# Modulation bundles moved between the stages of a two-block transformer kernel, and the values moved to the end of an attention step

## The chip, the cores and the metric

The kernel runs on one core of one Trainium2 chip. The metric is the device time of one execution in microseconds (us). Its parts are TensorE (PE in the profile, with PEld for its weight loads), VectorE (DVE), ScalarE (ACT), GpSimd (POOL) and SyncE (SP). SP issues the loads of the weights, POOL those of the modulation. All work is in fp32; most products are made of high and low parts of both operands, three products for one.

## What is computed

One sequence of 256 positions with 1024 features goes through two blocks.

```python
# block 1
h = rmsnorm(x, ln1)
qkv_a, z_a, b_a, a_a, q_b, k_b, v_b = split(h @ w_in)
y_a = gated_deltanet(qkv_a, z_a, b_a, a_a, ...)      # 4 heads of 128, chunks of 64, a triangular solve in each
y_b = dilated_attention(q_b, k_b, v_b)               # 8 heads of 64
x = x + concat([y_a, y_b]) @ w_out
h = rmsnorm(x, ln2)
x = x + (silu(causal_dwconv(h @ w_gate)) * (h @ w_up)) @ w_down      # 1024 -> 2816 -> 1024
x = rmsnorm(x, ln_f)
# block 2, layers i = 0 and 1
mod = silu(c) @ ada_w[i] + ada_b[i]                  # c [1, 1024], ada_w[i] [1024, 6144]
sh1, sc1, g1, sh2, sc2, g2 = split(mod, 6)
h = rms_norm(x, norm_mix_g[i]) * (1.0 + sc1) + sh1
y = diff_attention(h, ...) if i == 0 else chunked_attention(h, ...)   # 8 heads with 2 maps; 16 heads
x = x + g1 * y
h = rms_norm(x, norm_ffn_g[i]) * (1.0 + sc2) + sh2
x = x + g2 * grouped_moe(h, ...)                     # 16 experts of 512, 2 of them for each position
```

## The kernel before

**Units.** Every dense weight of block 1 and of the attentions goes through TensorE in units of 512 KB (128x1024 fp32). SP loads them six ahead: unit c waits until the low part of unit c-6 is made. ScalarE makes the high part (`whi`, L545), DVE the low part (`wlo`, L551), TensorE the products (L561). The units of `w_in` are those of Q and K (0 to 7), V, the gates G, and Z; `w_used` counts the units that TensorE is done with, and `U_V`, `U_FFN` and `U_WO` are the numbers at which the units of V, of the FFN and of the attention's output begin. The experts' weights of the MoE go through a ring of their own, without units.

**Bundles.** The product silu(c) @ ada_w of both layers doesn't depend on x. It is cut into 48 bundles, six groups of eight (8 chunks of the 1024 inputs). A bundle is 1 MB: `load_ada` issues two loads of 512 KB each on POOL's queue (L494). `ada_bundle` uses it in four matmuls of 128x512 whose output has 32 rows (eight records with the two passes of fp32, L506), summed in the bank `ADA_BANK[group]`. TensorE uses the bundles strictly in the order of their numbers, and `ada(to)` in its program means: all up to `to` now. Groups 0, 3 (g1 and g2 of a layer) end in `grow_add`, the others in `acol_copy`, a copy by ScalarE that frees the bank.

A bundle has a place, by the table of `ADA_PLACE`. Bundles 0 to 11 share two places in `ering`; the others up to `ADA_BLOCK` share three, the third of which is `a_raw`, laid over the tiles in which block 1's input of `w_out` is split (`a_hi`, `a_lo`). `load_ada` waits for `ada_used`, that is until the bundle that had the place before is used. Bundles from `ADA_BLOCK` on (`ADA_TAIL`) lie in places of the work buffer, which are free from the end of the delta rule on; places 13 and 14 are `a_raw` again.

```python
ADA_BLOCK = 24
ADA_TAIL = [0, 1, 2, 0, 1, 2, 0, 1, 2, 10, 11, 12, 0, 1, 2, 10, 12, 13, 14, 12, 13, 14, 12, 13]
ADA_PLACE = [n % (2 if n < ADA_LATE else 3) for n in range(ADA_BLOCK)] + ADA_TAIL
ADA_NORM, ADA_STEP, ADA_LASTS, ADA_FFN = 27, 30, 32, 40
```

**TensorE's order.** It is written out by hand, and so is that of the other engines; they meet at semaphores. Each engine runs its own list strictly in order. TensorE's, with times of the profile: the units of Q, K and V (10 to 60 us); the dilated attention (phase 0) with the units of G and bundles 0 to 5 beside it (to 121); Z with bundles 6 and 7 (to 141); the delta rule, whose triangular solve is a chain of small products, each waiting for DVE or ScalarE (144 to 199): bundles 8 to 13 stand ahead of its loop over the levels n = 1 to 5, 14 to 23 in it, two in each level; then the finale of the delta rule (L1819, L1825 and the groups of four `heads`, L1831; to 213) with no bundles; the turn of y (L718) and the eight units of `w_out` (L561, from 215.9); bundles 24 to 26 (`ADA_NORM`); the FFN's 22 steps (248 to 447), with bundles 27, 28, 29 behind steps 0, 1, 2, and 30 and 31 (`ADA_LASTS`) ahead of the last `down_pe`; bundles 32 to 39 (`ADA_FFN`) behind it; the last norm of block 1 and the turn 3 of its result; QKV of layer 0 (465 to 535); its attention, phase 1, one head in each of eleven overlapped steps (536 to 580), with bundles 40 to 47 one in a step; `w_o` (588 to 607), MoE (628 to 855); then layer 1 in the same way (856 to 1236). `busy(bank, 11)` (L1088) is eleven products of constants that only keep TensorE working; it stands ahead of turn 6, in layer 1 alone.

**POOL's order.** It issues bundles 0 and 1 once unit 3 has landed (`raw_in[3]`), then eight small loads of the bias rows (`grow`, L1592), then bundles 2 to 23, each at its wait. From the finale on: 24 to 29, `mod_spread(0)` (`mrow`, L1602), 30 to 35, the relative position tables (`t_rows`, `rel_rows`), 36 to 40, a mask (L1631), and when `w_o`'s units begin to be used up, 41 to 44; 45 to 47 stand between its partial sums of squares (L1642 to L1646) in the attention's last steps.

**DVE in phase 1.** A step of `attention_dve` has `largest(i)` (bias and maximum of both maps' scores, L933 to L938), `sums(i - 1)` (L958 to L964) and `values(i - 3)`: the division of the value product, which TensorE makes in L873, with its copy into `hn` (L980). `values` waits for that product (`pv_ps`). In phases 0 and 1 it stands at the head of the step, in phase 2 at its end.

## Time and profile before

| | |
|---|---|
| Median of the runs | 1237.31 us (1234.36, 1237.31, 1240.54) |
| Profiled execution, its own time | 1238.61 us |
| Span of the profiled execution | 1236.8 us, mean granted clock 0.978 |
| PE busy | 1111.0 us (90%) |
| PEld busy | 744.5 us (60%) |
| DVE busy | 593.5 us (48%) |
| ACT busy | 433.3 us (35%) |
| POOL busy | 94.7 us (8%) |
| Chain that ended last | PE 68%, DMA 16%, DVE 10%, ACT 4%, issue 2% |
| Bytes moved | 356.14 MB, mean 288 GB/s |

The profile is one execution. The busy time of an engine is an average over stages with different limits, so the chain that ended last, followed back from the last instruction, tells which work set the time in each stretch. In a row of a timeline the bracket is the idle time of the engine ahead of the instruction and what ended it. The records of one line that follow each other are drawn together (x8); when they overlap, the time is from the first start to the last end. PEclk is the granted clock of TensorE as a share of the full one.

### The profile page before, as it was taken

How to read it: one execution, taken by the hardware profiler on the slowest of the kernel's cores; microseconds unless marked ns; L12 is line 12 of the kernel's file. 1: busy time of each engine (PE TensorE's matmuls, PEld its weight loads, DVE VectorE, ACT ScalarE, POOL GpSimd, SP SyncE). 2: the span in 40 equal slices, each digit the busy share in tenths (PEclk: the TensorE clock that was granted, in tenths of full speed). 3: DMA queues.
4: the chain of work that ended last, by engine and by line, in shares of the span. 5: the costliest groups of instructions: out<-in, count | busy, mean ns of one | idle time of the engine just before them, and what ended most of it. 6: DMA issues, size and time to landing. Idle time of an engine off the chain costs nothing.

```text
span 1236.8 us, 17354 instructions
## 1 busy us (share of the span) xinstructions
PE 1111.0 (90%) x6770; PEld 744.5 (60%) x6770; DVE 593.5 (48%) x1175; ACT 433.3 (35%) x738; POOL 94.7 (8%) x189
## 2 busy tenths in 40 slices
PE   6899786999999989976999999987999999999986
PEld 6787455789999947844754343424887754343422
DVE  3378464566666647736532322225765532232223
ACT  5444522454455446435331120103545441020100
POOL 2010130232000010022000000001000000000000
PEclk9999999989999999988999999999999999999998
DMA  9855693799777774683579999997675479999995
GB/s 292 241 162 198 230 324 143 254 320 339 225 228 223 230 254 137 232 335 131 201 297 409 409 409 409 409 409 283 216 273 207 138 284 410 409 409 409 409 409 217
DMA packets 163983, 356.14 MB, mean 288 GB/s; under 512 B 10425, under 2 KB 79289, under 8 KB 163777
## 3 DMA queue, kind: packets, MB, share of 16 engines
q1 hardware_dynamic: 146864, 295.81, 65.9%
q0 software_dynamic: 17024, 59.26, 13.7%
q8 instruction: 51, 0.84, 0.3%
q14 instruction: 28, 0.22, 0.0%
q10 hardware_dynamic: 16, 0.02, 0.0%
HBM read 351.89 MB, written 7.36 MB: 290 GB/s over the span
## 4 chain that ended last, share of the span: by engine, by line
PE 68%; DMA 16%; DVE 10%; ACT 4%; issue 2%; POOL 0%; SPq 0%; DVEq 0%; ACTq 0%
PE bank L561 35%; PE bank L1112 12%; DMA ering<-in_moe_w_up 9%; PE bank L1123 8%; DMA a_raw<-in_ada_w 3%; PE bank L1080 3%; DVE wlo L551 2%; PE bank L506 2%; DMA wraw<-in_w_in 1%; DMA ering<-in_ada_w 1%; ACT whi L545 1%; PE bank L718 1%; PE bank L858 1%; PE bank L1184 1%; DVE work L2267 1%
## 5 line engine op out<-in xcount | busy, mean ns | idle before, releaser
L551 DVE TENSOR_TENSOR wlo<-wraw,whi 128x1024 fp32r<-128x1024 f32 x150 | 179.4, 1222 | 65.3 <-ACT whi L545 62.9
L545 ACT ACTIVATE whi<-wraw 128x1024 fp32r<-128x1024 f32 x150 | 153.9, 1054 | 60.9 <-PE bank L561 49.6
L561 PE MATMUL bank<-a_hi,whi 128*128 128x256 f32 x512 | 149.2, 291 | 5.8 <-DVE wlo L551 4.7
L561 PE MATMUL bank<-a_lo,whi 128*128 128x256 f32 x512 | 147.4, 288 | 0.0
L561 PE MATMUL bank<-a_hi,wlo 128*128 128x256 f32 x512 | 147.2, 288 | 0.0
L1112 PE MATMUL bank<-ering,work 128*64 128x512 f32 x592 | 134.0, 595 | 12.2 <-DMA ering<-in_moe_w_up 11.0
L1313 DVE TENSOR_TENSOR work<-work,bank 128x512 f32<-128x512 f32 x16 | 11.0, 688 | 208.7 <-PE bank L1112 208.7
L561 PEld LDWEIGHTS bank<-a_hi,whi 128*128 128x128 f32 x512 | 101.1, 197 | 14.0 <-issue 6.9
L561 PE MATMUL bank<-whi,a_hi 128*128 128x512 f32 x256 | 102.1, 399 | 5.7 <-DVE a_lo L748 3.0
L1221 ACT ACTIVATE o_hi<-work 128x512 fp32r<-128x512 f32 x32 | 20.2, 632 | 236.8 <-DVE work L1281 236.4
L1112 PEld LDWEIGHTS bank<-ering,work 128*64 128x64 f32 x592 | 41.2, 137 | 102.7 <-issue 79.7
L561 PEld LDWEIGHTS bank<-a_lo,whi 128*128 128x128 f32 x512 | 100.9, 197 | 0.7
L561 PEld LDWEIGHTS bank<-a_hi,wlo 128*128 128x128 f32 x512 | 100.8, 197 | 0.0
L561 PE MATMUL bank<-wlo,a_hi 128*128 128x512 f32 x256 | 100.5, 392 | 0.0
L561 PE MATMUL bank<-whi,a_lo 128*128 128x512 f32 x256 | 100.3, 392 | 0.0
L1123 PE MATMUL bank<-ering,work 128*64 128x512 f32 x352 | 78.5, 596 | 1.1 <-DVE work L1316 1.1
L1281 DVE SCALAR_TENSOR_TENSOR work<-bank,sm,mrow 128x512 f32<-128x512 f32 x32 | 22.6, 747 | 91.7 <-PE bank L1123 91.7
L561 PEld LDWEIGHTS bank<-whi,a_hi 128*128 128x128 f32 x256 | 48.4, 189 | 17.9 <-issue 7.4
L1209 ACT ACTIVATE work<-bank,mcol 128x256 f32<-128x256 f32 x64 | 31.6, 561 | 70.0 <-PE bank L1080 70.0
L561 PEld LDWEIGHTS bank<-whi,a_lo 128*128 128x128 f32 x256 | 48.5, 189 | 10.3
L561 PEld LDWEIGHTS bank<-wlo,a_hi 128*128 128x128 f32 x256 | 48.5, 189 | 9.8 <-issue 0.2
L1123 PEld LDWEIGHTS bank<-ering,work 128*64 128x64 f32 x352 | 24.2, 137 | 46.7 <-issue 44.4
(313 smaller groups left out, 1823.8 us busy)
## 6 DMA issues: line engine op xcount, KB each, us to landing
ering<-in_moe_w_down SPq DMA_DIRECT2D x44, 1024.0 KB, 18.4
ering<-in_moe_w_up SPq DMA_DIRECT2D x42, 1024.0 KB, 18.5
ering<-in_moe_w_gate SPq DMA_DIRECT2D x32, 1024.0 KB, 18.2
ering<-in_ada_w POOLq DMA_DIRECT2D x40, 512.0 KB, 5.8
work<-in_ada_w POOLq DMA_DIRECT2D x38, 512.0 KB, 7.5
work<-in_moe_w_gate SPq DMA_DIRECT2D x16, 1024.0 KB, 16.7
wraw<-in_w_in SPq DMA_DIRECT2D x28, 512.0 KB, 5.8
wraw<-in_a_w_qkv SPq DMA_DIRECT2D x24, 512.0 KB, 4.6
```

The costliest lines, as they stand in the source:

```text
L506: mm = nc.tensor.matmul(psum[ADA_BANK[g]][32 * q:32 * q + 32, :], silc[:, k, :], ada_part(n, q // 2)[:, (q % 2) * HALF:(q % 2 + 1) * HALF] ...
L545: nc.scalar.activation(w_hi(c), wraw[:, c % RING, :], ACT.Copy).then_inc(w_hi_done, 1)
L551: nc.vector.tensor_tensor(w_lo(u[0]), wraw[:, u[0] % RING, :], w_hi(u[0]).bitcast(F32), ALU.subtract).then_inc(w_lo_done, 1)
L561: mm = nc.tensor.matmul(out_ap, l, r, start=first and n == 0, stop=last and n == len(terms) - 1)
L718: tr = nc.tensor.transpose(turn_bank(turn, b)[:, (2 * kk + t) * P:(2 * kk + t + 1) * P], src[:, t, cols(2 * b + kk)], ident)
L858: tr = nc.tensor.transpose(psum[4 + n % 2][:, b * P:(b + 1) * P], scr[:, slot, b * P:(b + 1) * P], ident)
L1080: mm = nc.tensor.matmul(bank[:, kk * S:kk * S + cols], part[:, t, pair_cols(2 * b + kk)], sel[:, t, 0:cols // PAIR_SLOTS, :], start=n == 1 ...
L1112: mm = nc.tensor.matmul(bank[rows, :], x_e[:, k, rows], w[:, e, kk * HALF:(kk + 1) * HALF], start=first and kk == 0, stop=last and kk == 1)
L1123: mm = nc.tensor.matmul(psum[4 + half][rows, :], hid_t[:, m % 4, rows], w[:, e, half * HALF:(half + 1) * HALF], start=first, stop=last)
L1209: ins = nc.scalar.activation(xe[:, :, k, :], gather_bank(g, b)[:, kk * S:(kk + 1) * S].rearrange("p (a c) -> p a c", a=2), ACT.Identity, b ...
L1221: nc.scalar.activation(o_hi[:, cols], o_f[:, cols], ACT.Copy).then_inc(e_o_hi, 1)
L1281: return nc.vector.scalar_tensor_tensor(out=o_f[:, cols], in0=psum[4 + half][:, :], scalar=sm[:, M_GS:M_GS + 1], in1=mrow[:, 1, cols], op0 ...
```

## The change

- **Bundles 24 to 31 in block 1.** `ADA_BLOCK` is 32: these eight go through the three places of the ring too. TensorE's bundles 12 and 13 now stand behind the kk products, 14 and 15 behind m1, two in each level of the loop, 26 and 27 behind the products L1819 and L1825 (L1823 and L1830 in the changed file), 28 to 31 between the groups of heads.
- **Those behind move up.** `ADA_NORM` is 35, `ADA_LASTS` 37, `ADA_FFN` 40: 32 to 34 ahead of the FFN's norm, none between the FFN's steps, 35 and 36 ahead of the last `down_pe`, 37 to 39 behind it. `busy(psum[4], 11)` then stands ahead of the turn in layer 0 too. The attention keeps 40 to 47, one in a step.
- **Places and loads.** Bundle 41 gets a new place 15, which is `hn`, and is loaded when turn 3 has read `hn`. POOL loads 32 to 34 ahead of `mod_spread(0)`, 35 to 40 right behind it, 41 at the mask, 42 to 45 where 41 to 44 were, 46 and 47 between its sums.
- **First loads.** Bundles 0 and 1 wait for the eighth unit's products (`w_used` at `U_V`) and no longer for the landing of unit 3.
- **Banks and copies.** Group 3 sums in bank 7, group 4 in bank 2. `acol_copy(0)` stands ahead of the loop over the levels, `acol_copy(1)` at n = 5. `grow_add(1)` moves on DVE from the norm behind the FFN to block 1's turn, and TensorE waits for it ahead of the last bank of `w_out`'s first unit.
- **Values last.** In phase 1 `values(i - 3)` stands at the end of the step, as in phase 2.

```diff
@@ -122,14 +122,14 @@
 ADA_N = 8 * len(ADA_GROUPS)
-ADA_BANK = [7, 7, 7, 2, 3, 7]
+ADA_BANK = [7, 7, 7, 7, 2, 7]
 ADA_LATE = 12
-ADA_BLOCK = 24
-ADA_TAIL = [0, 1, 2, 0, 1, 2, 0, 1, 2, 10, 11, 12, 0, 1, 2, 10, 12, 13, 14, 12, 13, 14, 12, 13]
+ADA_BLOCK = 32
+ADA_TAIL = [0, 1, 2, 0, 1, 2, 10, 11, 12, 15, 13, 14, 12, 13, 14, 12]
 ADA_PLACE = [n % (2 if n < ADA_LATE else 3) for n in range(ADA_BLOCK)] + ADA_TAIL
-ADA_NORM, ADA_STEP, ADA_LASTS, ADA_FFN = 27, 30, 32, 40
+ADA_NORM, ADA_LASTS, ADA_FFN = 35, 37, 40
@@ -470,7 +470,7 @@
-            return {10: 3, 11: 4, 12: 5, 13: 3, 14: 4}.get(ADA_PLACE[n], ADA_PLACE[n])
+            return {10: 3, 11: 4, 12: 5, 13: 3, 14: 4, 15: 0}.get(ADA_PLACE[n], ADA_PLACE[n])
@@ -479,6 +479,8 @@
             place = ADA_PLACE[n]
+            if place == 15:
+                return hn[:, h, :]
             if place >= 3:
@@ -499,8 +501,8 @@
                 pe.wait_ge(grow_done, 1)
-            elif n == 16:
-                pe.wait_ge(acol_done, 1)
+            elif n in (16, 24):
+                pe.wait_ge(acol_done, n // 8 - 1)
             pe.wait_ge(ada_in[ada_ring(n)], 32 * ada_turn(n))
@@ -576,7 +578,7 @@
-        def unit_rows(pe, u, lhs_hi, lhs_lo, banks, first, last):
+        def unit_rows(pe, u, lhs_hi, lhs_lo, banks, first, last, last_bank=None):
@@ -584,6 +586,8 @@
                     h, l = w_hi(u[0])[:, cols], w_lo(u[0])[:, cols]
+                    if last_bank is not None and t + half == 2:
+                        last_bank()
                     mm = products(banks[t * 2 + half][:, :], [(lh, h), (lh, l), (ll, h)], first, last)
@@ -982,7 +986,7 @@
             for i in range(units + 3):
-                if ph < 2 and i >= 3:
+                if ph == 0 and i >= 3:
                     values(i - 3)
@@ -990,7 +994,7 @@
                     between(i)
-                if ph == 2 and i >= 3:
+                if ph != 0 and i >= 3:
                     values(i - 3)
@@ -1583,7 +1587,7 @@
-            pool.wait_ge(raw_in[3], 16)
+            pool.wait_ge(w_used, U_V)
             load_ada(pool, 0)
@@ -1605,11 +1609,11 @@
             nc.gpsimd.memset(fg[:, :, 0:2], 0.0).then_inc(pads_zero, 1)
-            for n in range(ADA_BLOCK, ADA_STEP):
+            for n in range(ADA_BLOCK, ADA_NORM):
                 load_ada(pool, n)
...
             mod_spread(0)
-            for n in range(ADA_STEP, ADA_STEP + 6):
+            for n in range(ADA_NORM, ADA_FFN + 1):
                 if ADA_PLACE[n] == 10:
@@ -1630,11 +1634,11 @@
-            for n in range(ADA_STEP + 6, ADA_FFN + 1):
-                load_ada(pool, n)
+            pool.wait_ge(tr_done, 4 * 4)
+            load_ada(pool, ADA_FFN + 1)
             toe_mask(0)
             pool.wait_ge(w_used, U_WO[0])
-            for n in range(ADA_FFN + 1, ADA_FFN + 5):
+            for n in range(ADA_FFN + 2, ADA_FFN + 6):
                 load_ada(pool, n)
@@ -1645,8 +1649,8 @@
                                         ).then_inc(sub_done, 1)
-                if ADA_FFN + 5 + n < ADA_N:
-                    load_ada(pool, ADA_FFN + 5 + n)
+                if ADA_FFN + 6 + n < ADA_N:
+                    load_ada(pool, ADA_FFN + 6 + n)
@@ -1772,7 +1776,7 @@
                 mm.then_inc(kk_ps, 1)
-            ada(13)
+            ada(14)
@@ -1780,7 +1784,7 @@
                 tr.then_inc(m1_ps, 1)
-            ada(14)
+            ada(16)
@@ -1805,12 +1809,12 @@
                     blocks(psum[3 * c], mb[c], ym[c]).then_inc(n_ps, 1)
-                ada(13 + 2 * n)
+                ada(15 + 2 * n)
                 for c in range(2):
...
                     blocks(psum[3 * c + 2], nm[c], xm[c]).then_inc(xyn_ps, 1)
-                ada(14 + 2 * n)
+                ada(16 + 2 * n)
@@ -1819,12 +1823,14 @@
                 mm.then_inc(n_ps, 1)
+            ada(27)
             for c in range(2):
...
                 mm.then_inc(xyn_ps, 1)
+            ada(28)
@@ -1834,14 +1840,18 @@
             heads(psum[6], lambda h: y_all[0][:, h, :], lambda h: bv[0][:, h, :], fin_ps)
+            ada(29)
             pe.wait_ge(fin_copied, 1)
...
             heads(psum[0], lambda h: aqk[0][:, h, :], lambda h: v0[:, h, :], fin_ps)
+            ada(30)
             pe.wait_ge(fin_copied, 2)
...
             heads(psum[2], lambda h: qkv_t[:, h, P:S], lambda h: s1[:, h, :], fin_ps)
+            ada(31)
             pe.wait_ge(fin_r, 1)
             heads(psum[3], lambda h: y_all[1][:, h, :], lambda h: r1[:, h, :], fin_ps)
+            ada(32)
             pe.wait_ge(fin_copied, 3)
@@ -1861,18 +1871,16 @@
                 chunk_ready(pe, 1, k)
-                unit_rows(pe, (U_WOUT + n, None, 0), a_hi[:, k, :], a_lo[:, k, :], psum[4:8], n == 0, n == KC - 1)
+                unit_rows(pe, (U_WOUT + n, None, 0), a_hi[:, k, :], a_lo[:, k, :], psum[4:8], n == 0, n == KC - 1,
+                          (lambda: pe.wait_ge(grow_done, 2)) if n == 0 else None)
             mod_columns(psum[3])
...
             step_pe(pe, 0, None, 0, turn=2)
-            ada(ADA_NORM + 1)
             step_pe(pe, 1, None, 0, first=True)
-            ada(ADA_NORM + 2)
             step_pe(pe, 2, None, 0)
-            ada(ADA_STEP)
@@ -1895,8 +1903,7 @@
                 pe.wait_ge(x_done, X_AT["ffn"] if l == 0 else X_AT["moe", 0])
-                if l == 1:
-                    busy(psum[4], BUSY_MOD)
+                busy(psum[4], BUSY_MOD)
                 turn = 3 + 3 * l
@@ -1919,7 +1926,6 @@
-                        pe.wait_ge(grow_done, 2)
                         pe.wait_ge(acol_done, 3)
@@ -2091,12 +2097,12 @@
                 nc.scalar.activation(dec[c], dec[c], ACT.Exp, scale=-1.0).then_inc(dec_exp, 1)
+            acol_copy(0)
             for n in range(1, len(LEVELS)):
-                if n in (2, LAST):
-                    acol_copy(0 if n == 2 else 1)
                 if n in (3, 4):
...
                 if n == 5:
+                    acol_copy(1)
                     for t in range(T):
@@ -2460,6 +2466,7 @@
             turn_lo(dve, 1, vec[:, V_Y1:V_Y1 + 8], EARLY)
+            grow_add(1)
             for c in range(2):
@@ -2538,8 +2545,6 @@
                     nc.vector.memset(v_one[:, :, :, 64:65], 1.0)
-                else:
-                    grow_add(1)
...
```

**TensorE, end of the delta rule.** L1800 is the last level's products; `ering` and `a_raw` are a bundle's places; L1819 and L1825 close the levels, L1831 is the finale, L718 the turn ahead of `w_out`. Before:

```order
L506 MATMUL bank<-ering,silc 32x512 x4
L1800 MATMUL bank<-work 64x64 x32
L506 MATMUL bank<-a_raw_55,silc 32x512 x2
L506 MATMUL bank<-a_raw_56,silc 32x512 x2
L1819 MATMUL bank<-work 64x64 x8
L1825 MATMUL bank<-work 64x64 x8
L1831 MATMUL bank<-work 128x128 x4
L1831 MATMUL bank<-work,mrow 128x128 x4
L1831 MATMUL bank<-work 128x128 x20
L718 MATMUL bank<-con,hn 128x128 x8
```

After (all lines are some lower in the file; L508 is the bundle):

```order
L1823 MATMUL bank<-work 64x64 x8
L508 MATMUL bank<-a_raw_55,silc 32x512 x2
L508 MATMUL bank<-a_raw_56,silc 32x512 x2
L1830 MATMUL bank<-work 64x64 x8
L508 MATMUL bank<-ering,silc 32x512 x4
L1837 MATMUL bank<-work 128x128 x4
L508 MATMUL bank<-ering,silc 32x512 x4
L1837 MATMUL bank<-work,mrow 128x128 x4
L1837 MATMUL bank<-work 128x128 x4
L508 MATMUL bank<-a_raw_55,silc 32x512 x2
L508 MATMUL bank<-a_raw_56,silc 32x512 x2
L1837 MATMUL bank<-work 128x128 x8
```

Where the finale had no bundle, six stand in or just ahead of it now (26 to 31; the last two follow below the rows).

**POOL, from the finale on.** `work`, `a_raw` and `hn` are the bundles' places, `mrow` the spread rows. Before:

```order
L1607 MEMSET work 128x2x2
L494 DMA work<-in_ada_w 128x1024 x12
L1602 DMA mrow<-grow_74 32x512 x16
L494 DMA work<-in_ada_w 128x1024 x12
L1620 DMA t_rows<-t_by_distance 128x512 x8
L1624 DMA rel_rows<-in_b_rel_bias 128x513 x16
L494 DMA work<-in_ada_w 128x1024 x10
L1631 MEMSET work 64x8x64
L494 DMA a_raw_55<-in_ada_w 128x1024 x2
L494 DMA a_raw_56<-in_ada_w 128x1024 x2
L494 DMA work<-in_ada_w 128x1024 x2
L494 DMA a_raw_55<-in_ada_w 128x1024 x2
```

After:

```order
L1611 MEMSET work 128x2x2
L496 DMA work<-in_ada_w 128x1024 x6
L1606 DMA mrow<-grow_74 32x512 x16
L496 DMA work<-in_ada_w 128x1024 x12
L1624 DMA t_rows<-t_by_distance 128x512 x8
L1628 DMA rel_rows<-in_b_rel_bias 128x513 x16
L496 DMA hn<-in_ada_w 128x1024 x2
L1635 MEMSET work 64x8x64
L496 DMA a_raw_55<-in_ada_w 128x1024 x2
L496 DMA a_raw_56<-in_ada_w 128x1024 x2
L496 DMA work<-in_ada_w 128x1024 x2
L496 DMA a_raw_55<-in_ada_w 128x1024 x2
```

Six loads (three bundles) stand ahead of the spread where twelve stood, twelve behind it, and the ten behind the tables are gone but for the two into `hn`.

**DVE, phase 1, end of its step 2 and start of its step 3.** L960 and L964 end the sums of a head, L980 is its values, L933 and L935 read the next scores. Before:

```order
L960 SCALAR_TENSOR_TENSOR sm_76<-sm_76 128x2
L964 SCALAR_TENSOR_TENSOR work_77<-work_77,sm_76 128x128
L964 SCALAR_TENSOR_TENSOR work_77<-work_77,sm_76 128x256
L980 TENSOR_TENSOR hn_67<-bank6,sm_76 128x2x128
L933 ISA work_77,sm_76<-bank2,work_77 128x128
L933 ISA sm_76 128x1
L935 ISA work_77,sm_76<-bank2,work_77 128x256
L935 ISA sm_76 128x1
```

After:

```order
L964 SCALAR_TENSOR_TENSOR sm_76<-sm_76 128x2
L968 SCALAR_TENSOR_TENSOR work_77<-work_77,sm_76 128x128
L968 SCALAR_TENSOR_TENSOR work_77<-work_77,sm_76 128x256
L937 ISA work_77,sm_76<-bank2,work_77 128x128
L937 ISA sm_76 128x1
L939 ISA work_77,sm_76<-bank2,work_77 128x256
L939 ISA sm_76 128x1
L942 TENSOR_SCALAR sm_76<-sm_76 128x2
```

The first values stood ahead of the scores of step 3; they now stand behind its sums. So at each border of steps DVE now does the values of the head before the one it did there.

## Rows read from the trace of the kernel before

**Rows 1.** The chain of waits, 169 to 200 us. Columns: start us, us, what.

```profile
169.52 6.43 DMA a_raw<-in_ada_w
...
177.91 9.70 DMA a_raw<-in_ada_w
...
189.57 8.80 DMA a_raw<-in_ada_w
198.41 1.07 PE bank L506 x8
```

**Rows 2.** Windows: stretch, length, busy PE, PEld, DVE, ACT, POOL, PEclk, DMA share, GB/s.

```profile
40.00:45.00 5.00, 5.00 (x34) 5.00 (x34) 2.81 (x3) 0.85 (x2) 0.00 (x0) 0.74 0.98 260
155.00:165.00 10.00, 8.99 (x88) 6.36 (x80) 6.92 (x15) 0.00 (x0) 3.82 (x8) 0.83 0.85 291
165.00:177.00 12.00, 10.24 (x226) 6.58 (x226) 6.71 (x18) 4.02 (x7) 3.53 (x7) 1.00 0.97 330
...
198.00:216.00 18.00, 11.63 (x105) 9.77 (x106) 9.27 (x19) 6.57 (x13) 0.00 (x0) 1.00 0.00 1
...
535.00:560.00 25.00, 15.72 (x110) 8.58 (x110) 12.60 (x68) 12.06 (x46) 9.16 (x18) 0.86 0.96 379
```

**Rows 3.** Timeline of TensorE: start, us, line, operation, tiles, xcount [idle before <-releaser].

```profile
39.56 0.55 PE L561 MATMUL bank<-a_hi,whi 128*128 128x256 f32 x1 [4.67 <-DVE wlo L551]
...
210.82 1.13 PE L1831 MATMUL bank<-work 128*128 128x128 f32 x8 [1.10 <-DVE sm L2451]
...
215.86 0.47 PE L561 MATMUL bank<-whi,a_hi 128*128 128x512 f32 x1 [3.04 <-DVE a_lo L748]
...
556.85 1.07 PE L506 MATMUL bank<-work,silc 128*32 128x512 f32 x8 [1.07 <-DMA work<-in_ada_w]
...
573.89 1.06 PE L506 MATMUL bank<-a_raw,silc 128*32 128x512 f32 x8
...
856.50 2.72 PE L1088 MATMUL bank<-con 128*128 128x128 f32 x22 [1.20 <-DVE x_res L1304]
```

**Rows 4.** The chain of waits over the whole run, columns as in Rows 1.

```profile
18.29 17.85 DMA wraw<-in_w_in
...
258.71 0.99 PE bank L506 x8
...
450.30 9.06 DMA work<-in_ada_w
...
465.06 22.01 PE bank L561 x96
...
859.39 1.16 ACT hn L660
...
863.93 22.01 PE bank L561 x96
```

**Rows 5.** DMA queue (packets, MB, share), 0 to 65 us; an issue, 66 to 68.

```profile
q0 software_dynamic: 832, 2.62, 12.4%
...
ering<-in_ada_w POOLq DMA_DIRECT2D x2, 512.0 KB, 4.3
```

**Rows 6.** Timeline of POOL, columns as in Rows 3.

```profile
14.51 2.26 POOL L494 DMA_DIRECT2D ering<-in_ada_w  x4 [12.67 <-DMA wraw<-in_w_in]
...
183.62 1.05 POOL L494 DMA_DIRECT2D ering<-in_ada_w  x2 [2.70 <-PE bank L506]
```

**Rows 7.** Timeline of DVE, columns as in Rows 3.

```profile
182.27 2.35 DVE L551 TENSOR_TENSOR wlo<-wraw,whi 128x1024 fp32r<-128x1024 f32 x2
...
212.06 0.69 DVE L2459 TENSOR_TENSOR work<-work,bank 128x512 f32<-128x512 f32 x1 [0.78 <-PE bank L1831]
...
555.81 0.42 DVE L980 TENSOR_TENSOR hn<-bank,sm 128x256 f32<-128x256 f32 x1 [1.31 <-PE bank L873]
...
560.32 0.42 DVE L980 TENSOR_TENSOR hn<-bank,sm 128x256 f32<-128x256 f32 x1 [1.31 <-PE bank L873]
```

**Rows 8.** Timeline of ScalarE, columns as in Rows 3.

```profile
454.52 1.15 ACT L660 ACTIVATE hn<-x_res,sm 128x1024 f32<-128x1024 f32 x1 [0.23 <-DVE sm L683]
```

## The prediction

> **What bounds the kernel now.** I read the chain of waits first, whole and then by stretch. It is TensorE's own work for 68% of the span and transfers for 16%, so I looked for the places in which the modulation bundles stand on it, since these are what the change moves. There are five. (1) In the delta rule's chain (166 to 199 us) one place of the bundle ring, `a_raw`, is all that counts: load, use, next load, three times over [rows 1]. In its first part TensorE is busy 10.24 of 12 us, the DMA share is 0.97 [rows 2]. Then comes the finale, in which no byte moves (198 to 216 us: 1 GB/s) [rows 2], and the first `w_out` unit at 215.86 [rows 3]. (2) At the start TensorE stands still for 4.67 us before unit 6 [rows 3], and the chain shows a transfer of 17.85 us that ends last [rows 4]. (3) In the FFN the chain is TensorE's work without a gap, so each bundle between the steps costs its own length, 0.99 us [rows 4]. (4) Behind the FFN eight bundles are done, and their transfers stand on the chain with 9.06 us [rows 4]. (5) In the first attention of block 2 bundle 43 is waited for 1.07 us [rows 3], and in each step of 4.51 us DVE waits 1.31 for TensorE's value products before it takes the next scores [rows 7].
>
> **Start: bundles 0 and 1 and the bias rows wait for unit 7.** POOL issues them from 14.5 us on [rows 6], among the first units of `w_in`. They are 2.62 MB and hold all 16 engines for 12.4% of 65 us, 8.06 us [rows 5]. Unit 7 lands at 36.14 (18.29 + 17.85) [rows 4]; behind it in ScalarE's and DVE's order stand the small split and unit 6's low part. With 8.06 us less ahead it lands at about 28. TensorE comes to unit 6 by its own work at 34.9 (39.56 - 4.67) [rows 3], so the whole stall goes, and the slow stretch behind it with it: the granted clock is 0.74 from 40 to 45 us [rows 2], 5 x 0.26 = 1.3. Sum -6.0. What is next: the same bytes come at about 41 us, beside units loaded six units ahead, and bundle 0 is used at 65. Ends -6.5 and -3.
>
> **Chain: bundles 24 to 31 in it.** TensorE's 1.07 us for each [rows 1] lies in the waits; what counts is the transfer. Bundles share three places, each loaded when the bundle three before is used. The hops of `a_raw` are 8.39 (169.52 to 177.91), 11.66 (to 189.57) and 10.71 us (to 198.41 + 1.07 + 0.8 for the next issue) [rows 1]. Three bundles pass in a hop: 2.80, 3.89, 3.57 us for one. In the second and the third a megabyte of weight units goes along, in the first none, and the late ones have none either (1 GB/s in 198 to 216) [rows 2]: I take 2.80, 22.4 for eight. By the rate of 165 to 177 us, 330 GB/s [rows 2], it would be 3.17 and 25.4. The earlier bundles are asked for sooner (two ahead of the level loop, where one stood), and from 155 to 165 us the share is 0.85 [rows 2], which is 1.5 us of room: with a little behind it 2 us. So the last one lands at 198.4 + 22.4 - 2 = 218.8. Behind it stand its own 1.07, one group of heads, the turn, `a_hi` and `a_lo`, 215.86 - 210.82 = 5.04 [rows 3]: `w_out` begins at 224.9, **+9.0**. At x us for a bundle the term is 8x - 13.4: +12.0 at 3.17, +17.8 at 3.89; below, 379 GB/s (535 to 560 us) [rows 2] is 2.77, and with 3 us of room +7.8. Queued behind each late bundle on TensorE are the heads, behind those ScalarE's copies and DVE's norm; all of the finale but its end is covered. `grow_add(1)` is one DVE operation like that of 0.69 us [rows 7] behind `a_lo`; TensorE asks for it only at the unit's fourth bank, after nine products: nothing.
>
> The row of 379 GB/s over 25 us [rows 2] can be set against a rule. The Trainium skill (page DMA: Bandwidth & Descriptors, section Where 436 GB/s comes from) says that a core's HBM side binds at about 358 GB/s. By that rule a bundle would be 2.93 us and the term +10.1; the row is above the page's figure, so the row stands.
>
> **FFN steps.** Three bundles between steps 0, 1 and 2 go, 0.99 us each [rows 4]: -3.0. TensorE remains the bound. Six bundles' loads now go out in one burst at about 243 to 250 us, 6.3 MB, 17 us at 370 GB/s, beside the FFN's first units. These are loaded six units ahead; I take no stall, and up to +3.
>
> **Behind the FFN.** After the last step's products three bundles are left, loaded long before, then eleven filler products (22 records, 2.72 us in the other layer) [rows 3], then the norm is next in line: ScalarE's half of `hn` ends at 454.52 + 1.15 = 455.67 [rows 8]. In the other layer, where only the norm stands ahead, the first unit begins 863.93 - 860.55 = 3.4 us behind it [rows 4]: here 459.06, against 465.06 [rows 4]. **-6.0**, ends -6.5 and -5.
>
> **First attention of block 2.** Bundle 41 lies in `hn` long before, so the transfers from 535 us on serve bundles 42 and later, each used one step later; they still come at the pace of the bytes, with a share of 0.96 [rows 2]. Bundle 44 comes when 43 came, 556.85 [rows 3], in step 4 and not in step 3. With the values last DVE doesn't wait 1.31 us in each step [rows 7]; 4.51 - 1.31 = 3.2, I take 3.3 for the handovers. Bundle 47 ends at 556.85 + 1.07 + 3 x 3.3 = 567.8, before at 573.89 + 1.06 = 574.95 [rows 3]: **-7.1**. The tail, in which POOL's partial sums now stand ahead of the last values, I leave as long as before, to 1 us. Ends -9 and -4. The MoE stages behind are paced by transfers that begin when `w_o` is done, so they move along.
>
> **Sum**, against the profiled execution (1238.61, span 1236.8): -6.0 + 9.0 - 3.0 - 6.0 - 7.1 = -13.1, 1225.5. The median of the runs, 1237.31, is 1.3 below it; the difference from that gives 1224.2, **1224**.
>
> **The rivals.** *A, dear bundles:* each costs 3.89 us as in the second hop, +17.8, the total is -4.3, **1233**. For it: two hops of three were of that size. Against it: the short one is the only one without other traffic. *B, gains taken back:* the moved loads stall the weight units at 41 and at 250 us, and the attention stays at the pace of its transfers past step 4: -2 + 9 + 0 - 6 - 4 = -3, **1234**. *C, slower, at the end of the delta rule:* the ring doesn't keep three loads in flight, because POOL's queue is held at the wait for the oldest place. A load alone lands in 4.3 us [rows 5]; with its second issue, the use and the handover 6.4 us if quite serial, +37.8 for the term and +15.7 in all, **1253**. It is slower from 4.4 us a bundle on, by over 0.5% from 5.2. Against it: three were in flight in every hop shown. *D, POOL is held by DVE:* if each of the 16 late issues waited for one DVE operation of 0.69 us [rows 7], 11 us come on top, **1235**. Against it: POOL's pair at 183.62 took 1.05 us [rows 6] while DVE ran two operations of 2.35 us with two inputs from the same memory [rows 7]. The Trainium skill (page SBUF — State Buffer, section SBUF: two separate sides) states such a lock: DVE's hold on the shared ports keeps POOL from writing descriptors. By that rule D would be the likely case; the pair's row doesn't show it. *E, every term at its good end:* -6.5 + 7.8 - 3 - 6.5 - 9 = -17.2, **1220**.
>
> **How the numbers follow.** Forecast 0.60, A 0.12, B 0.10, C 0.05, D 0.05, E 0.08. 0.5% is 6.2 us, about what a measurement of this kernel can tell from no change: faster ends at 1231.1, slower begins at 1243.5. Faster: forecast, E and a quarter of A and B, 0.73; slower: C and a little of B, 0.06; the rest, 0.21, is the same. The range holds forecast, E, A, B and D: **1217 to 1235**.
>
> **What the profile of the changed kernel would show.** Start: no idle time at unit 6. Chain: past bundle 23 hops of 8 to 9 us, with bytes where there were none, and `w_out` at about 219 (224.9 less the start's 6). FFN: no gap. Behind it: filler, and no transfer between FFN and turn. Attention: no idle time of DVE before the values, steps of 3.3 us. I am wrong if the late hops are over 10 us, if weight units stall at 41 or 250 us, or if the steps stay at 4.5.

## The result

The changed kernel takes 1223.34 us (median of 4 runs, 1221.25 to 1225.48) against 1238.92 us of the kernel before, measured beside it: a ratio of 0.9880, 95% interval 0.9846 to 0.9914, or 11 to 19 us less. By the half per cent that the prediction sets as its border this is faster. The forecast was 1224 us in a range of 1217 to 1235, and 13.1 us less. A second set of the changed kernel (`after_again`, 6 runs, median 1224.35) gave 0.9897 (0.987 to 0.9925); one execution of the kernel before in that set, of 3847.78 us, is left out of the ratio as a slow one.

The profiled execution took 1223.52 us, its span is 1221.7. On the page, the kind of chain hardly changed:

```profile
span 1221.7 us, 17399 instructions
...
PE 68%; DMA 15%; DVE 10%; ACT 4%; issue 2%; POOL 0%; SPq 0%; ACTq 0%; DVEq 0%; POOLq 0%
```

**By stage.** A stage ends where TensorE begins the next one (rows of its timeline and of the chain). Times are us. Both kernels were profiled twice; the second profiles are of `before_again` and `after_again` (below).

| Stage | before | before, second | after | after, second | forecast |
|---|---|---|---|---|---|
| to the first product of the gates | 141.15 | 142.68 | 134.89 | 134.36 | -6.0 |
| to the loop over the levels | 25.38 | 25.63 | 28.68 | 28.55 | |
| the loop | 32.88 | 33.91 | 33.70 | 35.62 | |
| finale and turn, to `w_out` | 16.45 | 16.46 | 21.35 | 21.13 | +9.0 (these three) |
| to the FFN's loop | 65.11 | 63.81 | 61.96 | 60.59 | -3.0 |
| the loop of the FFN | 161.59 | 161.59 | 161.59 | 161.60 | 0 |
| to QKV of layer 0 | 22.50 | 22.38 | 16.95 | 16.94 | -6.0 |
| QKV | 71.25 | 71.26 | 71.24 | 72.24 | 0 |
| attention, to its turn | 48.52 | 47.56 | 40.72 | 40.66 | -7.1 |
| from there to the MoE of layer 1 | 422.8 | 423.9 | 422.9 | 422.3 | 0 |
| the last MoE and the output | 229.18 | 229.04 | 227.73 | 226.63 | 0 |

**The chain of the changed kernel** (start us, us, what), against [rows 4]:

```profile
34.74 10.55 PE bank L563 x76
...
198.19 6.28 DMA ering<-in_ada_w
204.51 1.06 PE bank L508 x8
205.58 1.98 PE bank L1837 x16
207.56 0.99 PE bank L508 x8
208.56 1.98 PE bank L1837 x16
...
231.46 12.29 DMA wraw<-in_w_up
...
255.16 23.73 PE bank L563 x168
...
454.12 1.16 ACT hn L664
...
459.12 22.02 PE bank L563 x96
...
850.27 22.05 PE bank L563 x96
```

The transfer of 17.85 us at the start is gone; unit 6 starts at 34.74 with no idle time (the forecast said 34.9 for TensorE's own pace). Ahead of the FFN's norm a transfer of `w_up` now ends last, at 243.75; from the first unit of `w_out` to the FFN's first product it is 36.5 us instead of 36.0. The FFN's first steps are one piece, without bundles. QKV begins at 459.12, where the forecast had 459.06 with nothing moved ahead of the FFN's end; that end did move by only 0.4 us, since start, chain and FFN steps nearly cancel.

**Windows** (stretch, length, busy PE, PEld, DVE, ACT, POOL, PEclk, DMA share, GB/s), against [rows 2]: the slow stretch behind the start, the ring's stretch, and its end.

```profile
35.00:40.00 5.00, 5.00 (x44) 5.00 (x43) 1.67 (x2) 1.61 (x4) 0.00 (x0) 1.00 1.06 292
156.00:208.00 52.00, 41.96 (x704) 24.96 (x696) 21.18 (x46) 12.96 (x23) 17.38 (x34) 0.93 1.01 370
208.00:219.00 11.00, 7.96 (x66) 5.32 (x59) 8.17 (x14) 4.04 (x8) 0.00 (x0) 1.00 0.31 114
```

**TensorE's timeline at the end of the delta rule**, against [rows 3]. The idle time is in brackets, with what ended it.

```profile
194.26 2.08 PE L1804 MATMUL bank<-work 64*64 64x64 f32 x64 [1.37 <-ACT work L2114]
...
199.13 1.07 PE L508 MATMUL bank<-a_raw,silc 128*32 128x512 f32 x8 [0.43 <-DMA a_raw<-in_ada_w]
...
201.99 1.07 PE L508 MATMUL bank<-ering,silc 128*32 128x512 f32 x8 [0.72 <-DMA ering<-in_ada_w]
...
204.51 1.06 PE L508 MATMUL bank<-ering,silc 128*32 128x512 f32 x8 [0.36 <-DMA ering<-in_ada_w]
...
207.49 1.07 PE L508 MATMUL bank<-a_raw,silc 128*32 128x512 f32 x8
...
210.47 1.07 PE L508 MATMUL bank<-ering,silc 128*32 128x512 f32 x8
...
212.55 1.06 PE L508 MATMUL bank<-ering,silc 128*32 128x512 f32 x8
...
218.62 0.47 PE L563 MATMUL bank<-whi,a_hi 128*128 128x512 f32 x1 [3.04 <-DVE a_lo L752]
```

The rows from 199.13 on, but the last, are bundles 26 to 31. The last one that waits for its transfer is 28, at 204.51, and for 0.36 us. Bundles 29 to 31 lie ready. So in this profile, and in the second of the changed kernel, the ring sets the time up to about 205, and from there on it is TensorE's own order. In other profiles of the same delta rule bundles 30 and 31 are waited for too (a table below). The wait for ScalarE at 194.26 is new.

Ahead of the loop over the levels, the loop's first products in the kernel before, then bundle 15 and the same products in the changed kernel:

```profile
166.53 1.15 PE L1800 MATMUL bank<-work 64*64 64x64 f32 x32 [2.54 <-DVE work L2400]
```

```profile
161.71 1.93 PE L508 MATMUL bank<-ering,silc 128*32 128x512 f32 x8 [2.29 <-DMA ering<-in_ada_w]
163.57 1.83 PE L1804 MATMUL bank<-work 64*64 64x64 f32 x32
```

TensorE waited there for DVE; it now waits for bundle 15, and then bundle and products take 1.93 and 1.83 us instead of the 1.06 and 1.15 of other rows: the granted clock is 0.53 from 161.7 to 165.3 us. In the loop it is 0.63 from 185.2 to 189.8, behind a wait of 2.69 us for bundle 22.

### The profile page after: what moved, and what is told of

It is laid out like the page before. It is cut to its first block, busy times and chain, and to the rows that moved or that the text cites. A ratio compares the mean times of both kernels' runs of the same rounds, so it can differ in the third digit from the quotient of the medians.

```text
span 1221.7 us, 17399 instructions
## 1 busy us (share of the span) xinstructions
PE 1115.8 (91%) x6792; PEld 748.3 (61%) x6792; DVE 593.3 (49%) x1175; ACT 432.2 (35%) x738; POOL 94.5 (8%) x189
## 4 chain that ended last, share of the span: by engine, by line
PE 68%; DMA 15%; DVE 10%; ACT 4%; issue 2%; POOL 0%; SPq 0%; ACTq 0%; DVEq 0%; POOLq 0%
PE bank L563 35%; PE bank L1116 12%; DMA ering<-in_moe_w_up 9%; PE bank L1127 8%; DMA ering<-in_ada_w 3%; PE bank L1084 3%; PE bank L508 2%; DVE wlo L553 2%; DMA work<-in_ada_w 1%; ACT whi L547 1%; DMA wraw<-in_w_up 1%; PE bank L722 1%; PE bank L835 1%; PE bank L1188 1%; DVE work L2273 1%
## 5 line engine op out<-in xcount | busy, mean ns | idle before, releaser
L1116 PE MATMUL bank<-ering,work 128*64 128x512 f32 x592 | 134.0, 596 | 11.7 <-DMA ering<-in_moe_w_up 11.0
L563 PEld LDWEIGHTS bank<-whi,a_hi 128*128 128x128 f32 x256 | 48.5, 190 | 16.8 <-issue 6.4
L1213 ACT ACTIVATE work<-bank,mcol 128x256 f32<-128x256 f32 x64 | 31.6, 560 | 70.0 <-PE bank L1084 70.0
L563 PEld LDWEIGHTS bank<-wlo,a_hi 128*128 128x128 f32 x256 | 48.5, 190 | 9.8 <-issue 0.2
```

The costliest lines, as they stand in the source:

```text
L563: mm = nc.tensor.matmul(out_ap, l, r, start=first and n == 0, stop=last and n == len(terms) - 1)
L1116: mm = nc.tensor.matmul(bank[rows, :], x_e[:, k, rows], w[:, e, kk * HALF:(kk + 1) * HALF], start=first and kk == 0, stop=last and kk == 1)
L1213: ins = nc.scalar.activation(xe[:, :, k, :], gather_bank(g, b)[:, kk * S:(kk + 1) * S].rearrange("p (a c) -> p a c", a=2), ACT.Identity, b ...
```

## The experiments

Each is an edit of the changed kernel, unless its name says otherwise. Ratios are to the kernel before, measured beside the run.

**Is it the transfers? `few_bytes`**

```diff
+                cut = 8 if 24 <= n < 32 else D
-                nc.gpsimd.dma_start(ada_part(n, h), a["ada_w_2"][l][k * P:(k + 1) * P, j * D:(j + 1) * D]
+                nc.gpsimd.dma_start(ada_part(n, h)[:, 0:cut],
+                                    a["ada_w_2"][l][k * P:(k + 1) * P, j * D:j * D + cut]
```

> Bundles 24 to 31 load 8 of their 1024 columns (their sums are wrong by that), all else as in the changed kernel: the bytes of these eight are gone, TensorE's matmuls stay. Theory T (the transfers through the three places set the end of the delta rule): w_out begins 4 to 6 us earlier, at 213 to 215 instead of 218.6, and the last waits for bundles go; the rest of the 9.0 is TensorE's own time between the heads. Rival P (TensorE's own eight times 1.07 us set it, the transfers are hidden behind them): w_out begins within 1 us of 218.6.

Timeline of TensorE, the last two bundles and the first unit:

```profile
208.21 1.06 PE L510 MATMUL bank<-ering,silc 128*32 128x512 f32 x8
...
210.30 1.07 PE L510 MATMUL bank<-ering,silc 128*32 128x512 f32 x8
...
216.36 0.47 PE L565 MATMUL bank<-whi,a_hi 128*128 128x512 f32 x1 [3.04 <-DVE a_lo L754]
```

`w_out` begins at 216.36, 2.3 us before the changed kernel and 3.3 before its second profile; from the gates on it is 82.3 us against 83.7 and 85.3. The finale alone is 19.6 us instead of 21.3. Neither theory is right as it stood: by these profiles eight megabytes are worth 1.4 to 3 us, since TensorE's own order is close behind them. The part differs by as much from one profile of the changed kernel to the next, so only this is sure: they are not worth the 9.0. Median 1220.15, ratio 0.987 (0.9833 to 0.9908), which overlaps with the interval of `after_again` in the same set.

**And TensorE's part? `one_product`**

```diff
-            for q in range(4):
+            for q in ([3] if 24 <= n < 32 else range(4)):
```

> Bundles 24 to 31 keep all their bytes, but TensorE makes one of their four matmuls (three quarters of their sums are left out): 8 x 0.75 = 6 us less of TensorE. Theory T: the waits for the transfers take most of it, w_out begins 1 to 2 us earlier than 218.6. Rival P: 5 to 6 us earlier.

One of its bundles at the place of the one at 212.55:

```profile
213.27 1.04 PE L508 MATMUL bank<-ering,silc 128*32 128x512 f32 x2
```

The experiment didn't take away what it should. One matmul with an output of 32 rows lasts 1.04 us with its two passes; the four of a whole bundle last 1.06 us together. So they run side by side, each in another 32 rows of the output bank. 0.02 us of TensorE for each bundle was gone and not 0.75, `w_out` begins at 219.31, and the median is 1226.87 (0.9899). That agrees with what the Trainium skill (page TensorE: Matmul & The Clock Gate, section Part 3: Packing small matmuls — row/col tiling) says of matmuls whose outputs lie in different 32-row strips. The expectation had each of the four at a quarter of the bundle's time.

**What do the eight cost altogether? `neither`** has the edit of `few_bytes`, one matmul for each of these bundles, and 8 columns in it.

> Bundles 24 to 31 load 8 columns and TensorE makes one matmul of 8 columns for each instead of four of 512 (their sums are left out): what the eight cost in the chain altogether. Both theories: w_out begins 9.0 us earlier than in the changed kernel, at 209.6 (by the sum in the prediction). If it begins at 211 or later, part of the 9.0 was not the eight bundles, but the places and the moved copies.

`w_out` begins at 218.24, not at 209.6. Window of the finale, columns as above, and one of its groups of heads:

```profile
197.20:207.72 10.52, 9.58 (x58) 8.70 (x56) 1.28 (x4) 1.95 (x4) 3.88 (x8) 0.50 0.06 3
```

```profile
204.22 2.07 PE L1840 MATMUL bank<-work,mrow 128*128 128x128 f32 x8 [0.48 <-ACT work L2122]
```

With the bundles nearly gone the granted clock was 0.50 in this stretch, the lower of TensorE's two levels, and the same heads took 2.07 us that took 1.16 in the changed kernel, whose finale was granted 1.00. The finale was 21.8 us, and the gain was lost in it. Up to the finale nothing changed: 28.67 and 33.71 us in the two parts ahead of it, as in the changed kernel. So the 3.3 us ahead of the loop are no matter of bundles 24 to 31. Two more of the earlier ones stand ahead of it now, eight for six, and this is the likely reason, but no run takes them back alone. Median 1221.42, ratio 0.9878 (0.9843 to 0.9914). What the eight cost altogether this run can't say, since the clock took the gain.

**Is 16.45 us for the finale of before a chance? `before_again`** is the kernel before.

> The kernel before once more, for a second profile of its delta rule. Its finale took 16.45 us in the first profile, at a granted clock of 1.00. Theory C (that was a chance: without bundles in it the finale mostly runs at a lower clock, as in the other profiles without them): 19 us or more, clock 0.5 to 0.8. Theory T (it is 16.5 us as a rule, and the eight bundles made it 4.9 us longer): 16 to 17 us, clock 1.00.

Windows of the finale without bundles, in the kernel before, in its second profile, and in `before_values` (below), whose delta rule is the same:

```profile
199.40:215.90 16.50, 10.54 (x101) 9.51 (x97) 8.63 (x17) 6.57 (x13) 0.00 (x0) 1.00 0.00 0
```

```profile
202.20:218.70 16.50, 10.55 (x101) 9.50 (x97) 8.94 (x18) 6.56 (x13) 0.00 (x0) 0.99 0.00 0
```

```profile
200.30:219.60 19.30, 13.35 (x101) 12.20 (x97) 8.62 (x17) 6.56 (x13) 0.00 (x0) 0.82 0.00 0
```

Theory C falls: the finale is 16.5 us at the full clock in two of three. But the third had 0.82 and took 2.8 us more with the same instructions. The difference of 4.9 us between before and after is real, and one profile of this part is good to some 3 us.

**The finale over all profiles at a clock of 0.98 or more.** "Waits" is the sum of TensorE's waits for bundles in it.

| Profile | finale | waits | the rest |
|---|---|---|---|
| before, twice (no bundles) | 16.45, 16.46 | 0 | 16.45, 16.46 |
| changed, twice | 21.35, 21.13 | 1.51, 1.37 | 19.84, 19.76 |
| `hn_late` (below) | 21.39 | 1.72 | 19.67 |
| `start_early` (below) | 22.30 | 2.34 | 19.96 |
| `silu_early` (below) | 22.62 | 3.01 | 19.61 |
| `values_first` (below) | 23.17 | 3.45 | 19.72 |
| `few_bytes` | 19.62 | 0 | 19.62 |

The rest is the same within 0.4 us wherever the bundles' matmuls are. So six bundles cost TensorE's list 3.2 to 3.5 us here, about half of the 6.4 us that their rows add up to; the other half fills the waits of 0.51, 0.69, 0.62 and 1.10 us for DVE and ScalarE that the finale of before had between its groups of heads. The transfers add 1.4 to 3.5 us. The longest single wait is bundle 31's in `values_first`:

```profile
217.54 1.06 PE L508 MATMUL bank<-ering,silc 128*32 128x512 f32 x8 [2.37 <-DMA ering<-in_ada_w]
```

**Fewer bundles in the chain: `four_earlier`**

```diff
-SIDE_BUNDLES = [1, 1, 2, 2, 3, 3, 4, 4, 5, 6]
+SIDE_BUNDLES = [1, 2, 3, 3, 4, 5, 6, 6, 7, 8]
...
-                ada(min(7 + j, 8))
+                ada(9 + j)
...
-                ada(15 + 2 * n)
+                ada(19 + 2 * n)
...
-                ada(16 + 2 * n)
+                ada(20 + 2 * n)
...
+            grow_add(0)
             splits(U_WOUT)
```

`grow_add(0)` moves ahead of `splits(U_WOUT)` on DVE, `acol_copy(1)` to level 3 on ScalarE.

> Four bundles more are used ahead of the delta rule: eight instead of six in the dilated attention, four instead of two in the units of Z, all later places hold the bundle four numbers on, and the finale has none. Theory T: each costs its own 1.0 us in the attention and in Z (+4 to +5 with a wait in the ring of two places), and the chain, no longer held by the ring, ends 7 to 9 us earlier: total 3 to 5 us below the changed kernel. Rival P: the chain is shorter by the 1.07 us of each only, the total within 1 us of the changed kernel.

Timeline and window of its finale:

```profile
197.41 1.26 PE L508 MATMUL bank<-ering,silc 128*32 128x512 f32 x8 [2.22 <-DMA ering<-in_ada_w]
```

```profile
193.80:218.40 24.60, 16.93 (x116) 12.96 (x113) 9.22 (x18) 5.99 (x12) 0.00 (x0) 0.79 0.21 79
```

The part ahead of the loop is 26.5 us (28.7), the loop 31.6 (33.7), as theory T has it, although eight bundles (12 to 19) stand ahead of the loop here as well; the gates begin at 135.7, 1 us later. But the finale takes 24.6 us: bundle 30 is waited for by 2.22 us at its head, and the clock is 0.79. `w_out` begins at 218.42. Median 1223.53, ratio 0.9892 (0.9861 to 0.9922): no better than the changed kernel in the same set, `after_again`. The total is what rival P said, but not for its reason: the chain did get shorter ahead of the finale, and the finale took it back. The profile is of the fastest of its five executions, 1219.22 us.

> The changed kernel itself, as the measure for the three others of this set. Both theories: 1221 to 1226 us, 13 to 16 us below the kernel before.

`after_again` had a median of 1224.35 us, as expected.

**The new wait for ScalarE: `silu_early`**

```diff
+            for t in range(T):
+                act.wait_ge(z_evac, t + 1)
+                nc.scalar.activation(zs[:, t, :], zs[:, t, :], ACT.Silu).then_inc(z_evac, 1)
             acol_copy(0)
...
                 if n == 5:
                     acol_copy(1)
-                    for t in range(T):
-                        act.wait_ge(z_evac, t + 1)
-                        nc.scalar.activation(zs[:, t, :], zs[:, t, :], ACT.Silu).then_inc(z_evac, 1)
```

> The changed kernel with the Silu of z ahead of the loop over the levels on ScalarE, where it waits for a bundle anyway, and not behind the second acol_copy in level 5, where TensorE waits for ScalarE by 1.4 us. Theory S (the moved acol_copy pushes Silu and its 1.28 us of table load onto the path): the loop is 1.4 to 2.4 us shorter, 31.5 to 32.5 instead of 33.7 to 35.6, the total by as much. Rival (the bundles' transfers are late by the same anyway): no change, the wait moves to bundle 25 or 26.

TensorE's timeline, bundles 25 to 28:

```profile
198.05 1.06 PE L508 MATMUL bank<-ering,silc 128*32 128x512 f32 x8 [0.36 <-DMA ering<-in_ada_w]
...
201.04 1.06 PE L508 MATMUL bank<-a_raw,silc 128*32 128x512 f32 x8 [0.85 <-DMA a_raw<-in_ada_w]
...
203.57 1.07 PE L508 MATMUL bank<-ering,silc 128*32 128x512 f32 x8 [0.40 <-DMA ering<-in_ada_w]
...
206.66 1.06 PE L508 MATMUL bank<-ering,silc 128*32 128x512 f32 x8 [0.93 <-DMA ering<-in_ada_w]
```

The wait for ScalarE is gone, and these four wait 2.5 us for their transfers instead of 1.5 in the rows above. Bundle 31, at 215.60, waits 0.83 us more. The loop is 34.9 us. The rival holds: median 1224.06, ratio 0.9879 (0.9858 to 0.99).

**Both together: `two_earlier`** has the early Silu, the same side bundles as `four_earlier`, two bundles in Z, one less between the products ahead of the loop, and bundles 27 to 31 in the finale (26 to 31 in the changed kernel).

> As the last one, and two bundles more in the dilated attention, none more in Z; one bundle less stands between the products ahead of the loop, and one less in the finale, whose other bundles stay between the heads. Theory: +2 in the attention, the part ahead of the loop 1 to 3 us shorter (26 to 27), the finale keeps its clock and loses its waits (19 to 21): total 1 to 3 us below silu_early. Rival (the ring's pace sets the loop all the same, and the two bundles cost their 2 us): the same or 1 us above.

At the head of its finale:

```profile
201.01 1.93 PE L508 MATMUL bank<-ering,silc 128*32 128x512 f32 x8 [2.91 <-DMA ering<-in_ada_w]
```

The part ahead of the loop is 26.0 us, as expected. The finale isn't: a wait of 2.91 us, then a stretch at the lower level in which a bundle takes 1.93 us, 26.4 us in all. Median 1223.50, from 1217.60 to 1227.51, which is the profiled execution. Ratio 0.9872 (0.9846 to 0.9897). What I expected of the total is not shown.

**The start: `start_early`**

```diff
-            pool.wait_ge(w_used, U_V)
+            pool.wait_ge(raw_in[3], 16)
```

> The changed kernel with bundles 0 and 1 and the bias rows issued at the landing of unit 3 again. Theory of the prediction (their 2.62 MB stand ahead of unit 7, and nothing later depends on when they come): the 4.67 us ahead of unit 6 are back and the clock of 0.74 behind it, the end of the V units is 6.0 us later and so is everything behind it, total +6. Rival (the start's gain is partly taken back in the ring behind it, since the first bundles come later): total +3 or less.

```profile
40.01 0.55 PE L563 MATMUL bank<-a_hi,whi 128*128 128x256 f32 x1 [6.29 <-DVE wlo L553]
```

TensorE's wait ahead of unit 6 is back, with 6.29 us. The gates begin at 141.3 instead of 134.9 and 134.4, the chain from there takes 85.8 us (83.7 and 85.3), and the total is 1231.61, ratio 0.9943 (0.9924 to 0.9963). By the ratios that is 6 to 8 us more than the two of the changed kernel. The first theory holds; the ring behind gives nothing back.

**The attention: `values_first`, `before_values`, `hn_late`.** The first puts the values at the head of the step again:

```diff
-                if ph == 0 and i >= 3:
+                if ph < 2 and i >= 3:
```

> The changed kernel with the values of phase 1 at the head of the step again; bundle 41 still in its own place. Theory of the prediction (the pace of the last steps is DVE's wait for the value product, 1.31 us in each): steps 4 and on are 4.5 us again instead of about 3.2, the attention is 4 to 6 us longer. Rival (it is the bundle loaded ahead that shortens the attention, the order only moves the waits): 0 to 1 us longer.

The second is the kernel before with this edit the other way round:

> The kernel before with nothing changed but the values at the end of the step in phase 1. Theory of the prediction: bundle 43 is still waited for until 556.85, the steps behind it shrink to about 3.3 us, the attention is 3.5 to 5 us shorter. Rival (without the bundle loaded ahead the transfers set the pace): shorter by 1 us or less.

In the third the bundle's place stays and its load comes late:

```diff
-            load_ada(pool, ADA_FFN + 1)
             toe_mask(0)
             pool.wait_ge(w_used, U_WO[0])
-            for n in range(ADA_FFN + 2, ADA_FFN + 6):
+            for n in range(ADA_FFN + 1, ADA_FFN + 6):
```

> The changed kernel with bundle 41 still in its new place, but loaded with 42 to 45, when QKV is done. Theory of the prediction (the byte ahead is worth one step of the transfers): bundle 41 is waited for by 3 to 4 us again and the attention is 2 to 3 us longer than 40.7. Rival (the values' order alone made the gain): under 1 us longer.

DVE's timeline: the values in two steps of `values_first`, then of the changed kernel, against [rows 7]; last, bundle 41 on TensorE in `hn_late`.

```profile
565.73 0.42 DVE L984 TENSOR_TENSOR hn<-bank,sm 128x256 f32<-128x256 f32 x1 [1.31 <-PE bank L877]
...
570.23 0.42 DVE L984 TENSOR_TENSOR hn<-bank,sm 128x256 f32<-128x256 f32 x1 [1.31 <-PE bank L877]
```

```profile
557.17 0.42 DVE L984 TENSOR_TENSOR hn<-bank,sm 128x256 f32<-128x256 f32 x1
...
560.27 0.42 DVE L984 TENSOR_TENSOR hn<-bank,sm 128x256 f32<-128x256 f32 x1
...
562.52 0.41 DVE L984 TENSOR_TENSOR hn<-bank,sm 128x256 f32<-128x256 f32 x1
```

```profile
539.34 1.93 PE L508 MATMUL bank<-hn,silc 128*32 128x512 f32 x8 [4.68 <-DMA hn<-in_ada_w]
```

| | values | bundle 41 | attention | ratio |
|---|---|---|---|---|
| before, twice | first | late | 48.5, 47.6 | |
| `before_values` | last | late | 42.6 | 0.9968 (0.9942 to 0.9994) |
| `hn_late` | last | late | 44.0 | 0.9907 (0.9877 to 0.9936) |
| `values_first` | first | early | 45.5 | 0.9937 (0.9916 to 0.9959) |
| changed, twice | last | early | 40.7, 40.7 | 0.988, 0.9897 |

The wait of 1.31 us and the step of 4.50 us come back with the values at the head; without it the step is 3.1 us. The values' order is worth 4.8 us with the bundle ahead and 5 to 6 without, the bundle 2 to 3.3. Both theories of the prediction hold, both with a little more than expected, and the two parts add up to the 7 to 8 us.

## Why the prediction was right, and where it was only right in sum

- **Start, -6.0.** -6.3 in the first pair of profiles, -8.3 in the second, in which the kernel before stood still for 6.10 us and not 4.67. Over the four profiles with the early loads and eight with the late ones it is -6.8. The stall went whole, the clock behind it is 1.00, and no unit was late at 41 us (rival B). Right; the 4.67 us that it was built on was at the short end of 4.5 to 6.3.
- **Chain, +9.0.** 74.7 and 76.0 us of before, 78.4 in `before_values`: 76.4 on average. In the five with the changed delta rule (the two of the changed kernel, `hn_late`, `start_early`, `values_first`) 83.7, 85.3, 84.5, 85.8 and 87.7, 85.4 on average. That is +9.0 again, with a spread of 4 us in each group, and `w_out` at 218.62 stands where "at about 219" was written. The late hops of `a_raw` are 9.38 us (189.75 to 199.13) and 8.36 (to 207.49), in and near the 8 to 9 that were given and far from the 11.7 of rival A, which is out. **But the working was wrong in two steps.** First, "all of the finale but its end is covered": in the profiles of the changed kernel the ring's last wait is bundle 28's, the last load has landed when TensorE comes to it, and bundles 29 to 31 cost what TensorE and the heads take one after the other. The finale is 4.9 us longer: 1.5 us of waits for bundles and 3.4 of TensorE's own time for them (the table above), which I had put at nothing. Second, "a little behind it 2 us": asking for the earlier bundles sooner didn't give 2 us back, the part ahead of the loop is 3.3 us longer, and bundles 14 and 15 are now waited for in it. That this comes of the order is argued, not shown; `neither` shows only that it isn't bundles 24 to 31. The transfers were put too high and these two too low. A chain that needs 8 x 2.80 us of transfers and one that needs 3.3 + 0.8 + 4.9 gave the same figure, and that the errors cancel is luck; `few_bytes` tells the two apart, for by my formula all of the transfers' 9.0 but TensorE's part should have gone with the bytes, and 1.4 to 3 us did.
- **The page's rule of 358 GB/s** would have made the term +10.1. Over the 52 us of the window above the core moved 370 GB/s, so the row stands, as it did before the change. The rule is that of the Trainium skill (page DMA: Bandwidth & Descriptors, section Where 436 GB/s comes from), which gives it as a core's share of a stack that two cores use. This program runs on one core; its trace goes above the figure, and no run here has both cores at work.
- **FFN steps, -3.0.** -3.2 in both pairs of profiles. In the first pair the steps themselves are 3.6 us shorter, and the late unit of `w_up` ahead of them, which the forecast didn't have, takes 0.5 back. The burst of six loads at 246 us stalled nothing.
- **Behind the FFN, -6.0.** -5.5. Filler, norm, then QKV 3.84 us behind the norm's end (454.12 + 1.16) instead of 3.4.
- **Attention, -7.1.** -7.8 and -6.9. Bundle 44 is used at 550.81, where 550.9 follows from the forecast (556.85 less the 5.95 by which this part starts earlier), and the last one at 561.67, where it has 560.8 (567.8 less its own 1.06 and the 5.95). The steps between are 4.6, 3.2 and 3.1 us, where 3.3 was written for each: 6.3 us of the gain lie there, and 1.5 in the tail (9.4 us from the last bundle to the turn instead of 10.9), for which the forecast had nothing.
- **POOL held by DVE (rival D).** Every pair of issues for bundles 24 to 31 took 1.04 or 1.05 us, as in [rows 6]. The prediction's row of DVE is two operations in 2.35 us together. The lock of which the Trainium skill tells (page SBUF — State Buffer, section SBUF: two separate sides) holds there for DVE operations in a 2-port mode, and for those with two SBUF inputs only against a GpSimd operation that reads SBUF. So the prediction read too much into it when it called D the likely case by that rule: its row is of the second kind. The pairs of this case show no lock; they don't test the first kind.
- **What no term had.** The last MoE with the output is 1.45 us shorter in the first pair and 2.4 in the second. It was 226.8 us in `before_values` too, which has none of the moved bundles, and 229.5 in `few_bytes`, which has them all. So it moves by some 3 us whatever the kernel, and the 15.1 us of the first pair of profiles against 13.1 forecast are mostly this.
- **The new wait for ScalarE.** The forecast had nothing on the moved `acol_copy`. It puts a table load of 1.28 us and Silu on the chain; `silu_early` shows that it costs nothing in sum, as the transfers are as late.

None of the versions that compute the same beats the changed kernel by what can be measured. What stays open is what sets the clock in the finale: 1.00, 0.99 and 0.82 with no bundles in it; 0.98 to 1.00 in eight profiles with bundles between all heads; 0.72, 0.79 and 0.81 in `neither`, `four_earlier` and `two_earlier`. No run separates the length of a wait ahead of it from the work in it.

## What to carry to other kernels

When a resource (here the ring of three places) and the engine that uses it are nearly level, a term computed from the resource alone can have the right size and the wrong cause; write down both the time by the bytes and the time by the engine's own list, with each added operation in it, and take the later. Taking away the bytes alone and the work alone then shows which it was, but only if the work that is taken away really takes time: look first at whether the matmuls overlap. Work taken out of a stretch with many small waits may cost as much as it saves, since the clock can fall: one profile shows it (`neither`). That work put into such a stretch keeps the clock up is a guess that fits the finales above; no run shows it.

## What the hardware showed that I had not expected

- One fp32 matmul of 128x512 with 32 output rows takes 1.04 us (`one_product`), four of them in the four quarters of a bank take 1.06 us together. A bundle's price is that of one matmul.
- The finale with its bundles cut down to a matmul of 8 columns each (`neither`) ran at a granted clock of 0.50 for 10.5 us, and groups of heads of 1.16 us took 2.07. The same instructions in three profiles of the unchanged delta rule had 1.00, 0.99 and 0.82, which is 16.5 or 19.3 us.
- Values divided at the end of DVE's step and not at its head, with the same instructions, are worth 5 us over eight heads: DVE no longer stands 1.31 us in each step at the product that TensorE has just been given.
